# Strassen's scheme for 18 of the 22 k-tiles of each feed-forward down step, in a two-block fp32 transformer kernel on one core

## The chip, the core and the metric

The kernel runs on one core of a Trainium2 chip. The metric is the device time of one execution in microseconds. TensorE (PE) multiplies, VectorE (DVE), ScalarE (ACT) and GpSimd (POOL) do elementwise work, SyncE (SP) issues the DMAs. Each engine works through its own queue in program order, and semaphores tie the queues together.

## The reference

Two blocks of two layers each on 512 tokens of width 1024, all in fp32. What matters here is the last part of each layer:

```python
def conv_ffn(x, w_up, conv_k, conv_b, w_down):           # layers 0 and 1 of the first block
    h = x @ w_up                                         # 1024 -> 2 x 2816
    ...
    h = sum(hp[:, j:j + S] * conv_k[j] for j in range(CONV_W)) + conv_b
    a, b = jnp.split(h, 2, axis=-1)
    return (jax.nn.gelu(a, approximate=False) * b) @ w_down

def swiglu(xn, w_gate, w_up, w_down):                    # layers 0 and 1 of the second block
    return (jax.nn.silu(xn @ w_gate) * (xn @ w_up)) @ w_down
```

In the first block x = layer_norm(ALPHA * x + h) follows, in the second h + swiglu(...). The hidden width 2816 is 22 tiles of 128. The other stages (two mixers, cross attentions, a sparse attention, a convolution module) are not touched.

## The kernel before

**Precision.** Each fp32 operand is split into a high and a low part in the matmul's 32-bit format (`xh`, `xl`; `ah`, `al`; `wh`, `wl`), and each product is three matmuls: high x high, high x low, low x high. ScalarE makes the high part by a copy, VectorE the low part by a subtraction.

**The script.** `Script` writes one list of items; each engine's program goes through the list and does its own part of each item. So the order of the items is the order of every queue. Weights come in units of up to 1024 columns: SyncE loads a unit into one of 3 raw buffers (`weights`, L2391), `split` makes its parts in a ring of NR = 5 slots (L1430 on ScalarE, L1785 on VectorE, recorded at L1438/L1444 and L1792/L1798), and TensorE uses it in `mm` (L1182). `prefetch` (L209) puts the split of unit i + 4 into the list when unit i comes up; ScalarE then waits until unit i - 1 has been used. SyncE issues the load of a later raw unit only when `w_lo` of the present one has been made.

**PSUM.** There are eight banks of 128x512. `take` and `give` hand them out first in, first out; TensorE opens a bank only when its last reader has signalled (`free`).

**The feed-forward step** (`ffn`, L592). Stage numbers si are 2 and 5 in the first block (the conv form, called conv layers below) and 8 and 11 in the second (the gated form, gated layers). An up product `ups(m)` makes hidden tiles m and m + 1 (a pair) from four outputs of 128x512: 4 units of 24 matmuls. Its evacuation in a conv layer is ScalarE's tap (L1592), two taps on VectorE for each output (L2033, L2036), a Gelu, and two products (L2043); then ScalarE makes the hidden tiles' high parts (L1602) and VectorE their low parts (L2048), in `ah` and `al`. In a gated layer ScalarE applies Silu (L1611) and VectorE multiplies (L2056). The order is: six up products; `residual` over hidden tiles 0 to 9; five up products; `residual` over tiles 10 to 21. `residual` (L333) goes through the two halves of the 1024 output columns, four token tiles each, and adds each finished 128x512 sum into `x` (L1995, a first one with ALPHA at L1992). The last half goes token tile by token tile over its last three units, so that layer norms (L1812 to L1821) and transposes (L1196) of the first tiles start early. `by_tiles` (L367) does this for both halves in the cross attention.

## Time and profile before

| | us |
|---|---|
| median of 3 runs | 3467.57 (3466.55 to 3467.74) |
| profiled execution, its own span | 3464.9 |
| TensorE busy | 3404.4 |
| VectorE busy | 1870.3 |
| ScalarE busy | 1401.5 |
| GpSimd busy | 252.1 |
| DMA, mean rate | 91 GB/s |

The busy time of TensorE counts overlapping matmuls once, so its share says whether the queue had work, not how fast that work went. The four feed-forward stages take about 350 us each. Times inside a stretch are from the span's start. PEclk 1.00 is 2.4 GHz.

### The profile page before, as it was taken

How to read it: one execution, taken by the hardware profiler on the slowest of the kernel's cores; microseconds unless marked ns; L12 is line 12 of the kernel's file. 1: busy time of each engine (PE TensorE's matmuls, PEld its weight loads, DVE VectorE, ACT ScalarE, POOL GpSimd, SP SyncE). 2: the span in 40 equal slices, each digit the busy share in tenths (PEclk: the TensorE clock that was granted, in tenths of full speed). 3: DMA queues.
4: the chain of work that ended last, by engine and by line, in shares of the span. 5: the costliest groups of instructions: out<-in, count | busy, mean ns of one | idle time of the engine just before them, and what ended most of it. 6: DMA issues, size and time to landing. Idle time of an engine off the chain costs nothing.

```text
span 3464.9 us, 41693 instructions
## 1 busy us (share of the span) xinstructions
PE 3404.4 (98%) x16871; PEld 2849.4 (82%) x16871; DVE 1870.3 (54%) x3030; ACT 1401.5 (40%) x2489; POOL 252.1 (7%) x319
## 2 busy tenths in 40 slices
PE   9999999999999999999999999999999999999999
PEld 8888888888888888888888777888888887888887
DVE  5644566646565545676455695553333696543332
ACT  4543233424235333334243554544232565543231
POOL 1300210000032002000001020100000000100000
PEclk9999999999999999999999999999999999999999
DMA  4111342322331123423232222412222302313222
GB/s 160 56 55 62 109 158 73 104 97 92 98 105 60 49 86 114 141 68 103 98 98 77 75 71 90 132 57 96 98 97 98 104 28 90 105 55 108 95 96 79
DMA packets 89330, 315.13 MB, mean 91 GB/s; under 512 B 10673, under 2 KB 11441, under 8 KB 88625
## 3 DMA queue, kind: packets, MB, share of 16 engines
q1 hardware_dynamic: 89136, 312.46, 27.4%
q8 instruction: 133, 2.18, 0.3%
q14 instruction: 61, 0.49, 0.0%
HBM read 308.23 MB, written 4.19 MB: 90 GB/s over the span
## 4 chain that ended last, share of the span: by engine, by line
PE 88%; DVE 7%; ACT 2%; POOL 2%; issue 1%; DMA 0%; SPq 0%; DVEq 0%; ACTq 0%; POOLq 0%
PE bk L1182 76%; PE bk L1276 3%; PE bk L1240 2%; PE bk L1250 1%; PE bk L1196 1%; DVE ar L2165 1%; DVE wl L1792 1%; DVE st L2163 1%; PE bk L1367 1%; PE bk L1365 1%; PE bk L1366 1%; POOL x L2354 1%; POOL st L2286 1%; DVE x L1821 0%; DMA wr<-in_wpk 0%
## 5 line engine op out<-in xcount | busy, mean ns | idle before, releaser
L1182 PE MATMUL bk<-xh,wh 128*128 128x512 f32 (+1 forms) x2216 | 837.8, 378 | 5.1 <-DVE xl L1805 5.1
L1182 PE MATMUL bk<-xh,wl 128*128 128x512 f32 (+1 forms) x2216 | 830.3, 375 | 0.0
L1182 PE MATMUL bk<-xl,wh 128*128 128x512 f32 (+1 forms) x2216 | 829.6, 374 | 0.0
L1792 DVE TENSOR_TENSOR wl<-wr,wh 128x1024 fp32r<-128x1024 f32 (+1 forms) x372 | 449.4, 1218 | 660.7 <-ACT wh L1438 659.7
L1438 ACT ACTIVATE wh<-wr 128x1024 fp32r<-128x1024 f32 (+1 forms) x372 | 385.8, 1046 | 706.4 <-PE bk L1182 653.6
L1182 PEld LDWEIGHTS bk<-xh,wh 128*128 128x128 f32 x2216 | 417.5, 188 | 78.6 <-DVE wl L1798 3.8
L1182 PEld LDWEIGHTS bk<-xh,wl 128*128 128x128 f32 x2216 | 417.2, 188 | 75.3
L1182 PEld LDWEIGHTS bk<-xl,wh 128*128 128x128 f32 x2216 | 417.6, 188 | 72.0
L1182 PE MATMUL bk<-wh,ah 128*128 128x512 f32 x1184 | 466.6, 394 | 4.5 <-DVE al L2250 2.9
L1182 PE MATMUL bk<-wh,al 128*128 128x512 f32 x1184 | 461.7, 390 | 0.0
L1182 PE MATMUL bk<-wl,ah 128*128 128x512 f32 x1184 | 461.3, 390 | 0.0
L1798 DVE SCALAR_TENSOR_TENSOR wl<-wr,par,wh 128x512 fp32r<-128x512 f32 (+1 forms) x360 | 249.4, 738 | 308.2 <-ACT wh L1444 306.9
L1444 ACT ACTIVATE wh<-wr,par 128x512 fp32r<-128x512 f32 (+1 forms) x360 | 236.1, 708 | 335.8 <-PE bk L1182 328.8
L1182 PE MATMUL bk<-wh,xh 128*128 128x512 f32 (+1 forms) x768 | 295.6, 385 | 6.3 <-DVE wl L1792 6.3
L1182 PE MATMUL bk<-wh,xl 128*128 128x512 f32 (+1 forms) x768 | 289.4, 377 | 0.0
L1182 PE MATMUL bk<-wl,xh 128*128 128x512 f32 (+1 forms) x768 | 289.2, 377 | 0.0
L1182 PEld LDWEIGHTS bk<-wh,ah 128*128 128x128 f32 x1184 | 222.5, 188 | 51.9 <-issue 3.6
L1182 PEld LDWEIGHTS bk<-wh,al 128*128 128x128 f32 x1184 | 222.4, 188 | 46.5
L1182 PEld LDWEIGHTS bk<-wl,ah 128*128 128x128 f32 x1184 | 222.6, 188 | 45.5 <-issue 0.7
L2286 POOL TENSOR_SCALAR st<-st 128x1 f32<-128x1 f32 (+3 forms) x97 | 48.6, 502 | 2434.6 <-DVE st L1814 988.3
L1276 PE MATMUL bk<-ar 128*128 128x64 f32 (+2 forms) x1168 | 176.1, 286 | 11.9 <-ACT ar L1531 7.6
L1182 PEld LDWEIGHTS bk<-wh,xh 128*128 128x128 f32 x768 | 146.9, 191 | 34.1 <-DVE wl L1792 6.7
(276 smaller groups left out, 4095.5 us busy)
## 6 DMA issues: line engine op xcount, KB each, us to landing
wr<-in_wpk SPq DMA_DIRECT2D x540, 512.0 KB, 3.4
gb<-in_ln_g SPq DMA_DIRECT2D x6, 512.0 KB, 4.5
gb<-in_ln_b SPq DMA_DIRECT2D x6, 512.0 KB, 6.0
ar<-in_xT SPq DMA_DIRECT2D x8, 256.0 KB, 6.5
wr<-in_wpk SPq DMA_DIRECT2D x8, 256.0 KB, 6.0
ar<-in_memT SPq DMA_DIRECT2D x2, 1024.0 KB, 5.0
x<-in_x SPq DMA_DIRECT2D x4, 512.0 KB, 5.3
park<-x SPq DMA_DIRECT2D x4, 512.0 KB, 6.2
```

Of the source, the lines that this page charges most:

```text
L1182: i = pe.e.matmul(dst, lw, rw, start=g not in opened, stop=end)
L1196: i = pe.e.transpose(ps[:, tile(q)], src[:, tile(j + q)], ident)
L1240: ins = pe.e.matmul(ps[:, 0:w], lw, rw, start=q == 0, stop=q == len(pairs) - 1)
L1250: ins = pe.e.transpose(ps[:, tile(q)], src[:, tile(q)], ident)
L1276: ins = pe.e.matmul(ps[:, col:col + A.dv], src[:, tile(q)], val, start=q == 0, stop=k == k1 - 1)
L1365: pe.e.matmul(ps[:, :], dh, oh[:, j:j + 512], start=j == 0, stop=False)
L1366: pe.e.matmul(ps[:, :], dh, ol[:, j:j + 512], start=False, stop=False)
L1438: act.e.activation(m.wh[:, s, 0:nk * cols], m.wr[:, r, 0:nk * cols], ACT.Copy) \
L1444: act.e.activation(m.wh[:, s, a], m.wr[:, r, a], ACT.Copy, scale=m.p(gain[0], gain[1] + kk, 1)) \
L1792: dve.e.tensor_tensor(m.wl[:, s, a], m.wr[:, r, a], m.wh[:, s, a].bitcast(F32), ALU.subtract) \
L1798: i = dve.e.scalar_tensor_tensor(m.wl[:, s, a], m.wr[:, r, a], m.p(gain[0], gain[1] + kk, 1), m.wh[:, s, a].bitcast(F32), ALU.mult, ALU.su ...
L2286: pool.e.tensor_scalar(out, var, scale, eps, ALU.mult, ALU.add).then_inc(*ev.up("pool_ev"))
```

## The change

Hidden tiles 0 to 17 (nine pairs, three phases of three pairs) are multiplied with their weights by seven products in place of eight; a product takes two token tiles, one k-tile combination and 512 columns. Each product has two units: the first with two pairs (12 matmuls), the second with the third pair (6). The order is 1, 2, 5, 6, 3, 7, 4. Four pairs of banks (a to d) hold the sums: products 6 and 7 are added to 1's banks and 3 to 5's, after each state has been read; `sev` adds a state of a bank to one quarter of `x`, or to two (product 7). The combinations of weights (`combo`, T1 to T4) and of the hidden state (`comb`) are made on VectorE. The down weights of the 18 tiles come by `down_load`, 1 MB for a pair, into `wd`, and no longer through the raw ring; the loads of a phase stand in the up product before it, at its last three steps. `hid_hi` and `hid_lo` make the hidden state's parts from a queue `soon`; a pair's seven blocks are 1792 columns. The products' units are put between the units of the next up products: two behind the second, third and fourth unit of a phase's first up product, two behind each unit of its second, and in the third phase three behind some. The last two pairs (tiles 18 to 21) follow in `last_pairs`, both halves, token tile by token tile. The core of the diff:

```diff
+LEFT = {1: 0, 5: 4, 2: 2, 6: 5, 3: 6, 7: 1, 4: 3}
+RIGHT = {1: 0, 5: 1, 2: 2, 6: 1, 3: 3, 7: 0, 4: 2}
+COMBO = {5: "T1", 6: "T2", 7: "T3", 4: "T4"}
+ORDER = (1, 2, 5, 6, 3, 7, 4)
+HOME = {1: "a", 6: "a", 7: "a", 5: "b", 3: "b", 2: "c", 4: "d"}
+PART = {1: ((0, 0),), 5: ((1, 1),), 2: ((0, 0),), 6: ((0, 1),), 3: ((0, 1),), 7: ((1, 1), (1, 0)), 4: ((1, 0),)}
+AFTER = {6: 1, 7: 6, 3: 5}
...
+        units = self.plan or self.units
+        while self.split < min(i + 1 + LOOK, self.rel + NR, len(units)):
+            if units[self.split][0] == "seven":
+                _, F, q, c = units[self.split]
+                for pair in F.chunks[c] if q in COMBO else ():
+                    self.add("combo", F, COMBO[q], pair)
             self.add("split", self.split)
...
+    def seven(self, F):
+        n = len(F.chunks)
+        for q in ORDER:
+            if HOME[q] not in F.home:
+                F.home[HOME[q]] = [self.take(), self.take()]
+            for c in range(n):
+                F.slot[q, c] = self.use(("seven", F, q, c))
+                self.add("smm", F, q, c)
+                self.rel += 1
+                self.prefetch(F.slot[q, c])
+                if c < n - 1:
+                    yield
+            for tt in range(2):
+                self.add("sev", F, q, tt)
+                if q in (2, 3, 7, 4):
+                    self.give(F.home[HOME[q]][tt])
+            yield
...
+        def part(t, u):
+            for G in halves:
+                if u == 0:
+                    G.grp.append(self.take())
+                    if t == 0:
+                        G.unit[0] = self.use((0, 2, G.pieces, None))
+                elif t == 0:
+                    G.unit[1] = self.use((2, 2, G.pieces, None))
+                self.add("mm", G, u, [t], None, t == NT - 1)
+                if t == NT - 1:
+                    self.rel += 1
+                    self.prefetch(G.unit[u])
+        def finish(t):
+            if si == 11:
+                for hf, G in enumerate(halves):
+                    self.add("ev", G, t)
+                    self.give(G.grp[t])
+                    self.add("store", hf, t)
+                return
+            self.add("ev", halves[0], t)
+            self.give(halves[0].grp[t])
+            if t < 2:
+                self.close(si, t)
+            elif t == 2:
+                self.turn_x(si, 0)
+                self.leave(2)
+        for t in range(2):
+            part(t, 0)
+        yield
+        for t in range(2):
+            part(t, 1)
+            finish(t)
+            yield
+        for t in range(2, NT):
+            for u in range(2):
+                part(t, u)
+            finish(t)
+            yield
+        if si != 11:
+            late = [("ln", si, 2), ("turn", si, 2), ("norm", si, 3)] if si in (2, 5) else \
+                [("ln", si, 2), ("norm", si, 3), ("turn", si, 2)]
+            self.rest = [("turn", si, 1)] + late + [("turn", si, 3)]
...
-        for m in range(0, 12, 2):
-            drive((ups(m), 1))
-        drive((self.residual(si, down, [l, 0], 10, "hid", norm=False), 1))
-        for m in range(12, 22, 2):
-            drive((ups(m), 1))
-        drive((self.residual(si, down, [l, 10], 12, "hid", first=False, base=10), 1))
+        def made(pair, seven=None, per=(0, 0, 0, 0), after=0, loads=None):
+            for step, _ in enumerate(ups(2 * pair)):
+                if loads is not None and step in (1, 2, 3):
+                    self.add("down_load", *loads, 3 * loads[0].ph + step - 1, l)
+                if seven is None:
+                    if self.soon:
+                        self.add(*self.soon.pop(0))
+                elif step < 2 and pair % 3 == 0 and self.soon:
+                    self.add(*self.soon.pop(0))
+                for _ in range(per[step] if seven else 0):
+                    next(seven, None)
+            if pair < 9:
+                self.add("comb", si, pair)
+            self.soon += [("hid_hi", si, pair), ("hid_lo", si, pair)]
+        F = [Seven(si, ph, range(3 * ph, 3 * ph + 3)) for ph in range(3)]
+        made(0)
+        made(1, loads=(F[0], None))
+        made(2)
+        for ph in range(3):
+            products = self.seven(F[ph])
+            pair = 3 * ph + 3
+            made(pair, products, (0, 2, 2, 2) if ph < 2 else (0, 3, 3, 2))
+            if ph < 2:
+                made(pair + 1, products, (2, 2, 2, 2))
+                drive((products, 1))
+                made(pair + 2, loads=(F[ph + 1], F[ph]))
+            else:
+                held, self.soon = self.soon, []
+                steps = ups(2 * pair + 2)
+                for step in range(4):
+                    next(steps)
+                    if step < 2:
+                        for _ in range(3):
+                            next(products, None)
+                    if step == 1:
+                        drive((products, 1))
+                        self.soon = held
+                    elif self.soon:
+                        self.add(*self.soon.pop(0))
+                drive((steps, 1))
+                self.soon += [("hid_hi", si, 10), ("hid_lo", si, 10)]
+        while self.soon:
+            self.add(*self.soon.pop(0))
+        drive((self.last_pairs(si, down, l), 1))
...
+    def smm(F, q, c):
+        j = F.slot[q, c]
+        pe.wait_ge(*ev["w_lo", j])
+        for tt in range(2):
+            g = F.home[HOME[q]][tt]
+            ps = bk[sc.bank[g]]
+            if g not in opened:
+                begin(g)
+            if q in AFTER:
+                pe.wait_ge(*ev["sev", F.si, F.ph, AFTER[q], tt])
+            for kk, pair in enumerate(F.chunks[c]):
+                pe.wait_ge(*ev["hid", F.si, pair])
+                a = slice(tt * 128, tt * 128 + 128)
+                hh, hl = (m.hid(side, pair, LEFT[q], 256)[:, a] for side in (m.hh, m.hl))
+                wh, wl = (side[:, j % NR, kk * 512:kk * 512 + 512] for side in (m.wh, m.wl))
+                whole = c == len(F.chunks) - 1 and kk == len(F.chunks[c]) - 1
+                for n, (lw, rw) in enumerate(((hh, wh), (hh, wl), (hl, wh))):
+                    i = pe.e.matmul(ps[:, :], lw, rw, start=g not in opened, stop=whole and n == 2, skip_group_check=True)
+                    opened.add(g)
+            names = [("grp7", F.si, F.ph, q, tt)] if whole else []
+            if tt:
+                names.append(("used", j))
+            if names:
+                i.then_inc(*ev.up("mm", *names))
...
+    def split_seven(j):
+        _, F, q, c = sc.units[j]
+        act.wait_ge(*ev["used", j - NR])
+        for pair in F.chunks[c]:
+            act.wait_ge(*ev[(COMBO[q], F.si, pair) if q in COMBO else ("d_sw", F.si, pair)])
+        n = F.at(c)[1]
+        act.e.activation(m.wh[:, j % NR, 0:n * 512].rearrange("p (k c) -> p k c", k=n), m.right(F, q, c), ACT.Copy) \
+            .then_inc(*ev.up("w_hi", ("w_hi", j, 0)))
+    def hid_hi(si, pair):
+        if pair >= 3:
+            act.wait_ge(*ev["grp7", si, pair // 3 - 1, 4, 1])
+        if pair >= 9:
+            for p in range(2):
+                act.wait_ge(*ev["prod", si, 2 * pair + p])
+            act.e.activation(m.hid(m.hh, pair, 0, 1024), m.z(si, pair), ACT.Copy) \
+                .then_inc(*ev.up("x_hi", ("hid_hi", si, pair)))
...
+    def comb(si, pair):
+        z, zx = heads(m.z(si, pair), 4), heads(m.zx[pair % 2], 3)
+        for p in range(2):
+            dve.wait_ge(*ev["prod", si, 2 * pair + p])
+        if pair >= 2:
+            dve.wait_ge(*ev["hid", si, pair - 2])
+        dve.e.tensor_tensor(zx[:, 0, :], z[:, 1, :], z[:, 3, :], ALU.add).then_inc(*ev.up("dve_ev"))
+        own()
+        dve.e.tensor_tensor(zx[:, 1, :], zx[:, 0, :], z[:, 0, :], ALU.subtract).then_inc(*ev.up("dve_ev"))
+        dve.e.tensor_tensor(z[:, 1, :], z[:, 0, :], z[:, 1, :], ALU.subtract).then_inc(*ev.up("dve_ev"))
+        own()
+        dve.e.tensor_tensor(zx[:, 2, :], z[:, 2, :], zx[:, 1, :], ALU.subtract) \
+            .then_inc(*ev.up("dve_ev", ("comb", si, pair)))
+    def hid_lo(si, pair):
+        dve.wait_ge(*ev["hid_hi", si, pair])
+        i = dve.e.tensor_tensor(m.hid(m.hl, pair, 0, 1024), m.z(si, pair), m.hid(m.hh, pair, 0, 1024).bitcast(F32),
+                                ALU.subtract)
+        if pair >= 9:
+            i.then_inc(*ev.up("x_lo", ("hid", si, pair)))
+            return
+        dve.e.tensor_tensor(m.hid(m.hl, pair, 4, 768), m.zx[pair % 2], m.hid(m.hh, pair, 4, 768).bitcast(F32),
+                            ALU.subtract).then_inc(*ev.up("x_lo", ("hid", si, pair)))
+    def combo(F, name, pair):
+        w = m.wd[:, F.pairs.index(pair)]
+        dst, x, y = {"T1": (1, 1, 0), "T2": (1, 3, 1), "T3": (0, 1, 0), "T4": (2, 2, 1)}[name]
+        if name == "T1":
+            dve.wait_ge(*ev["d_sw", F.si, pair])
+        else:
+            dve.wait_ge(*ev["w_lo", F.slot_of({"T2": 5, "T3": 1, "T4": 2}[name], pair)])
+            dve.wait_ge(*ev["T1" if name == "T2" else "T2", F.si, pair])
+        dve.e.tensor_tensor(w[:, dst, :], w[:, x, :], w[:, y, :], ALU.subtract) \
+            .then_inc(*ev.up("dve_ev", (name, F.si, pair)))
+    def sev(F, q, tt):
+        ps = bk[sc.bank[F.home[HOME[q]][tt]]]
+        dve.wait_ge(*ev["grp7", F.si, F.ph, q, tt])
+        names = [("sev", F.si, F.ph, q, tt)]
+        if q in (2, 3, 7, 4):
+            names.append(("free", F.home[HOME[q]][tt]))
+        for n, (half, hf) in enumerate(PART[q]):
+            t = 2 * half + tt
+            xs = m.x[:, t, hf * 512:hf * 512 + 512]
+            marks = names if n == len(PART[q]) - 1 else []
+            own()
+            if F.si < 6 and F.ph == 0 and (q in (1, 5, 6) or (q, hf) == (7, 0)):
+                i = dve.e.scalar_tensor_tensor(xs, xs, ALPHA, ps[:, :], ALU.mult, ALU.add)
+            else:
+                i = dve.e.tensor_tensor(xs, xs, ps[:, :], ALU.add)
+            i.then_inc(*ev.up("dve_ev", *marks))
...
+    def down_load(F, before, pair, l):
+        n = F.pairs.index(pair)
+        if before is None:
+            sp.wait_ge(*ev["act", F.si, 0])
+        else:
+            sp.wait_ge(*ev["w_lo", before.slot_of(4, before.pairs[n])])
+        sp.e.dma_start(m.wd[:, n].rearrange("p b c -> p (b c)"), ins["wdn"][(F.si // 6 * 2 + l) * 9 + pair, :, :]) \
+            .then_inc(*ev.up(f"d_sw{n}", ("d_sw", F.si, pair), by=16))
```

On SyncE `split` and `weights` skip the units of the products; ScalarE's evacuation of a conv up product waits for the low part two pairs back, as before. `lay_out` packs the down weights of tiles 0 to 17 as pairs.

## Rows read from the trace of the kernel before

**Rows 1.** The page's first part: busy time, share of the span, instructions of each engine.
```profile
span 3464.9 us, 41693 instructions
...
PE 3404.4 (98%) x16871; PEld 2849.4 (82%) x16871; DVE 1870.3 (54%) x3030; ACT 1401.5 (40%) x2489; POOL 252.1 (7%) x319
```

**Rows 2.** The page's chain that ended last, shares of the span by engine.
```profile
PE 88%; DVE 7%; ACT 2%; POOL 2%; issue 1%; DMA 0%; SPq 0%; DVEq 0%; ACTq 0%; POOLq 0%
```

**Rows 3.** Waits of TensorE, whole span: total us, times, longest us.
```profile
PE bk L1196 <- DVE x L1821: 7.7, 8, 1.2
...
PE bk L1182 <- DVE wl L1792: 6.6, 3, 5.7
```

**Rows 4.** Stretches, a conv and a gated feed-forward: length, busy us, clock, DMA share, GB/s.
```profile
591.00:940.00 349.00, 348.96 (x1602) 291.45 (x1600) 188.49 (x226) 125.83 (x155) 3.62 (x4) 1.00 0.31 101
...
2355.00:2690.00 335.00, 335.00 (x1508) 278.79 (x1507) 122.02 (x161) 104.96 (x150) 0.47 (x2) 1.00 0.30 99
```

**Rows 5.** Timeline of TensorE in a down step: start us, us, instruction; 33 matmuls apart.
```profile
2500.06 0.39 PE L1182 MATMUL bk<-wh,al 128*128 128x512 f32 x1
...
2507.54 0.39 PE L1182 MATMUL bk<-wh,al 128*128 128x512 f32 x1
```

**Rows 6.** Timeline of VectorE, evacuation of one conv up product and two splits.
```profile
646.57 0.74 DVE L2033 SCALAR_TENSOR_TENSOR ar<-bk,par,ar 128x511 f32<-128x511 f32 x1
...
652.49 1.29 DVE L2043 TENSOR_TENSOR ar<-ar 128x512 f32<-128x512 f32 x2
...
655.43 2.36 DVE L1792 TENSOR_TENSOR wl<-wr,wh 128x1024 fp32r<-128x1024 f32 x2 [0.26 <-ACT wh L1438]
```

**Rows 7.** Groups of VectorE by form, whole span: count, busy us, mean ns, idle before.
```profile
L1792 DVE TENSOR_TENSOR wl<-wr,wh 128x1024 fp32r<-128x1024 f32 x364 | 444.0, 1229 | 654.2 <-ACT wh L1438 653.2
...
L1995 DVE TENSOR_TENSOR x<-x,bk 128x512 f32<-128x512 f32 x80 | 54.8, 685 | 63.7 <-PE bk L1182 61.2 <-DVE x L1995 0.5
...
L1870 DVE TENSOR_TENSOR al<-bk,ah 128x256 fp32r<-128x256 f32 x16 | 6.8, 425 | 0.5
```

**Rows 8.** ScalarE: two groups by form, whole span, and one row of its timeline.
```profile
L1438 ACT ACTIVATE wh<-wr 128x1024 fp32r<-128x1024 f32 x364 | 380.8, 1055 | 699.2 <-PE bk L1182 653.6 <-DMA wr<-in_wpk 45.5
...
L1602 ACT ACTIVATE ah<-ar 128x512 fp32r<-128x512 f32 x44 | 27.2, 633 | 51.8 <-DVE ar L2043 51.8
...
645.64 0.78 ACT L1592 ACTIVATE ar<-bk,par 128x512 f32<-128x512 f32 x1 [0.24 <-PE bk L1182]
```

**Rows 9.** The page's DMA issues: count, KB each, median us from issue to landing.
```profile
wr<-in_wpk SPq DMA_DIRECT2D x540, 512.0 KB, 3.4
...
ar<-in_memT SPq DMA_DIRECT2D x2, 1024.0 KB, 5.0
```

**Rows 10.** A stretch at the kernel's start, its last column the GB/s.
```profile
8.00:12.00 4.00, 4.00 (x12) 3.15 (x11) 3.11 (x5) 2.42 (x4) 0.00 (x0) 1.00 1.06 412
```

**Rows 11.** Waits of TensorE from 930 to 975, the end of a conv layer.
```profile
PE bk L1196 <- DVE x L1821: 2.2, 2, 1.2
```

**Rows 12.** Stretches in attention; the third number from the right is the granted clock.
```profile
114.40:117.40 3.00, 1.63 (x11) 1.26 (x12) 2.59 (x9) 2.45 (x5) 2.83 (x4) 1.00 0.00 0
117.40:120.80 3.40, 2.70 (x10) 2.01 (x9) 1.74 (x5) 1.74 (x5) 3.22 (x4) 0.50 0.44 124
...
1059.50:1062.90 3.40, 3.40 (x10) 2.63 (x9) 2.18 (x5) 2.11 (x6) 1.25 (x2) 0.50 0.37 145
```

**Rows 13.** Timeline of TensorE at the kernel's start, 12 matmuls between the last two rows.
```profile
5.67 0.79 PE L1182 MATMUL bk<-wh,xh 128*128 128x512 f32 x1 [5.67 <-DVE wl L1792]
6.26 0.63 PE L1182 MATMUL bk<-wl,xh 128*128 128x512 f32 x1
...
11.38 0.50 PE L1182 MATMUL bk<-wl,xh 128*128 128x512 f32 x1
```

More of the change, by code:

```diff
@@ L193, in __init__ @@
         self.last_gate, self.last_branch, self.conv_g = {}, {}, None
+        self.soon = []
         self.build()
+        self.raws = [j for j, d in enumerate(self.units) if d[0] != "seven"]
+        self.raw = {j: r for r, j in enumerate(self.raws)}
     def add(self, *item):
@@ L211, in prefetch @@
             return
-        n = len(self.units) if self.total is None else self.total
-        while self.split < min(i + 1 + LOOK, self.rel + NR, n):
+        units = self.plan or self.units
[4 more added lines that the diff above has]
+                    self.add("combo", F, COMBO[q], pair)
             self.add("split", self.split)
@@ L1455, in rms @@
         else:
-            act.wait_ge(*ev["res", si, 1, t])
+            for hf in range(2):
+                act.wait_ge(*ev["res", si, hf, t])
         if t >= 2 and si > 5:
@@ L2407, in split @@
     def split(j):
-        if j + NRAW < len(sc.units):
+        if j in sc.raw and sc.raw[j] + NRAW < len(sc.raws):
             sp.wait_ge(*ev["w_lo", j])
-            weights(j + NRAW)
+            weights(sc.raw[j] + NRAW)
     def row(name, l, n):
```

116 lines of the change are left out of this document (72 added, 44 removed).

## Prediction

> **What bounds the kernel now.** I read the busy table first: TensorE is busy for 3404.4 of 3464.9 us, VectorE for 1870.3, ScalarE for 1401.5 [rows 1]. The chain that ended last agrees: 88% of it is TensorE [rows 2]. The list of who waited for whom shows how little TensorE waits for others: the two largest causes are 7.7 and 6.6 us [rows 3]. So removed matmuls pay, but only as far as the other queues keep pace, and the next view is the table of the feed-forward stretches. In the first block's ones (conv, si 2 and 5) VectorE works 188.5 of 349 us and ScalarE 125.8; in the second block's (gated, si 8 and 11) 122.0 and 105.0 of 335 [rows 4]. TensorE has no gap in either. A 512-column matmul there follows the one before it after (2507.54 - 2500.06) / 33 = 0.2267 us [rows 5]; its listed 0.39 us is latency, not price. A unit of 24 matmuls thus lasts 5.44 us, and an up product (4 units) 21.8 us.
>
> **What is removed.** Before, 9 pairs of k-tiles in the down step cost 9 x 2 x 8 x 3 = 432 matmuls in each of 4 layers; seven products on two token tiles cost 9 x 7 x 2 x 3 = 378. So 54 x 0.2267 = 12.24 us a layer, **49.0 us in all**. The last 4 of 22 k-tiles keep their count.
>
> **What is added, by price.** Matmul forms are the same. On VectorE, per layer: 36 differences of weights (T1 to T4) of 128x512, which follow each other after 0.60 us (two end within 1.29 [rows 6]); 36 differences of the hidden state at 256 columns, 0.42 us each by the nearest form, 9 x 1.6 = 14 us [rows 7]; low halves for 1792 instead of 1024 columns a pair, 9 x 0.85 = 8 us; 46 weight splits (25 full at 1.13 us in a row, 21 half at 0.60 [rows 6]) instead of 22, +16 us; 48 + 8 readings of sums into x instead of 16, each 0.69 [rows 7] plus the wait on its own queue, 0.72, +29 us. With 22 us for the weights this is about +89 us a layer: 188 to 277 of some 340 us in the conv layers, 122 to 211 in the gated ones. On average there is room. The order decides, so I walked one phase (3 pairs) through the in-order queues.
>
> VectorE's lead is the ring of 5 split weights: unit i+4 is split while TensorE works on unit i. A product has only two units, of 12 and 6 matmuls (2.72 and 1.36 us), so four units of lead shrink from 21.8 us to 13.6 to 16.3. For products 4 to 7 the split is serial: differences (1.2 us), ScalarE's copy 1.06 (half: 0.63 [rows 8]), VectorE's subtraction 1.15.
>
> **Conv layers, first phase.** Time 0 is the start of the first woven up product. The first woven up lasts with its 3 products to 34.0, the second with 4 products to 72.1, the free third to 93.8. VectorE is idle last near 24, then it works to the end of the second: 7.2 us for each up product's taps and products (646.57 to 653.8 [rows 6]), 11 splits, 14 sum readings of 0.72, 9 differences, 1.6 us of hidden differences. It frees the first bank that the second woven up reuses at about 31.9, where TensorE asks at 34.0; it splits the unit asked for at 43.5 by 40.7. These margins of 2 to 3 us hold, so **no stall** inside (estimate; 0 to 3 us a phase is the bound). But it lags: it splits the second unit of the next phase's first up at 82.3, where an unburdened queue would at 79.9.
>
> **Change of phase.** SyncE's in-order queue passes that split, then issues one weight transfer and at once all three 1 MB transfers of the next phase's weights: the units between are products, for which it doesn't wait. One 512 KB transfer lands after 3.4 us, a 1 MB one after 5.0 [rows 9], and at 412 GB/s [rows 10] a further 1 MB takes 2.6, by the difference in rows 9 3.2. The second lands at 82.3 + 3.4 + 2 x (2.6 to 3.2) = 91 to 92, the third at 93.5 to 95.3. ScalarE meets the splits of these weights at 83 and stands; behind them in its queue is the evacuation of the third up, whose first bank is complete at 89.8. That starts 4 to 6 us late. From the third landing: copy 0.6, tap 0.8, VectorE's 7.2, low half of the pair before 2.0, hidden differences 1.6, high half 1.85, a weight copy 1.0 and its split 1.15, low half 2.0: 18.2 us, so 111.7 to 113.5. TensorE asks for this pair in the first product's second unit, at 107.4. **Stall 4.3 to 6.1, taken 5.3**, twice a layer; without the transfers it would be about 0.1. In the gated layers the same walk has 79.8 for SyncE, no taps, and ends at 105.1, before 107.4: no stall.
>
> **Third phase.** Its weave puts the second product's last unit right ahead of product 5, which takes the banks that product 2 gives back. VectorE reads them only behind two differences and a split. TensorE asks 1.36 us after the unit's start; the readings end 2.3 us too late in conv layers (1.5 to 3), 1.8 in gated ones (1.2 to 2.4).
>
> **Ahead of the last two pairs.** The low half of pair 9 stands in VectorE's queue behind pair 10's evacuation, and the first matmul after that up asks for it. In the trace the first output's tap begins at 645.64, a quarter into the last unit [rows 8], so the up ends near 649.6, the products end at 653.8, and the low half needs another 1.15: **5.4 us** (5.0 to 6.0). Gated: one multiply 0.7, low half 1.15, signals: 2.1 (1.8 to 2.6). Pair 10 itself is ready at +6.5, behind 5.44 us of matmuls that start at +5.4: hidden.
>
> **The tail by token tile.** From the first tile's end to its transposes there are 36 matmuls, as before. VectorE has one reading and its statistics more for each tile; the present order waits 2.2 us in that place [rows 11]. I take +1 in the two conv layers (0 to 2) and nothing in the gated ones, the last store included.
>
> **TensorE's clock.** The table of stretches shows a granted clock of 1.00 (2.4 GHz) from 114.4 to 117.4, while TensorE was busy 1.63 of 3 us, and 0.50 (1.2 GHz) over the next 3.4; another fall lasts 3.4 us in all [rows 12]. At the kernel's start the matmuls behind a pause of 5.67 us follow each other after (11.38 - 6.26) / 12 = 0.427 us [rows 13], and only from 11.4 on at the full pace. So a fall of 3.4 us costs 3.4 x (1 - 0.2267 / 0.427) = 1.6 us. The six pauses of over 5 us (three in each conv layer) can each be followed by one: 0 to 9.6 us, taken at 6.4 (four of six). The Trainium skill, page "TensorE: Matmul & The Clock Gate", section "HAM oscillation — how this bites in real kernels", says that long idle gaps between groups of matmuls put the array back to its low clock. By that rule all six would be paid, and the sum would be 3 us higher.
>
> A second rule speaks against the change: the skill's page "VectorE: DVE Perf Modes", section "The TRN2 errata — SBUF-src ops pay a fixed extra latency per instruction", has small operands pay the same fixed part as large ones. The trace has it: 0.42 us for 256 columns and 0.69 for 512 [rows 7]. With the page's formula, (N + 151) / 0.96 ns, an estimate for the four hidden differences of a pair is 1.7 us instead of 1.6, which changes nothing.
>
> **The sum.** Conv layer: 2 x 5.3 + 2.3 + 5.4 + 1 = 19.3, two layers 38.6. Gated: 1.8 + 2.1 = 3.9, two 7.8. Clock 6.4. Together 52.8 lost against 49.0 removed: +3.8 us. The profiled execution spans 3464.9 us, the median of the three runs shown is 3467.6, 2.7 us longer, and I keep that distance: **3471 us**. With all lower ends (8.6 a phase pair, 1.5, 5.0, 0; gated 3.0; no clock) the loss is 36.2 us and the time 3455, with all upper ones (12.2, 3, 6, 2; gated 5.0; 9.6) it is 66 and 3485.
>
> **Rivals.** *The gain is kept.* If ScalarE meets the new weights already landed, the phase stall falls to 0.1 (minus 20.8 us), and with it most of the clock term (minus 5) and the tail (minus 2): 3443 us. For it: my walk gives VectorE's lag to within a microsecond or so, and the three transfers would only need to be issued 5 us earlier. Against it: SyncE's place behind that split is in the code. Chance 0.33 for this and what lies between (3438 to 3462).
> *VectorE becomes the bound.* In the second woven up of every conv phase the margin is 2.1 us at the first reused bank. A phase adds 44 instructions in VectorE's queue up to 72 (12 differences, 14 product splits, 14 readings, 4 of the hidden state). If each costs 0.12 us more than here, for a handshake with ScalarE or a wait on its own queue, that is 5.3 us a phase, of which the margin takes 2.1: 3.2 x 6 phases = 19, so 3490 us, slower. It decides from 2.1 / 44 = 0.05 us an instruction. For it: every price here was seen on a VectorE about half busy. Against: back to back instructions in rows 6 run closer than their listed time. Chance 0.25 (3479 to 3500).
> The forecast, 3462 to 3479, has 0.38; 0.04 lies outside. That the change doesn't do what it says I leave out: the matmul count is fixed by the code.
>
> What a measurement of this kernel can tell from no change is about 0.2%, 7 us. Faster by more (under 3460.6): the first rival, almost whole, and an edge of the forecast, 0.35. Slower by more (over 3474.5): the second and a part of the forecast, 0.32. Between: 0.33. The range that leaves out 2 in 10 runs from 3441 to 3489; the likeliest case's own from 3462 to 3479.
>
> **What would show it.** 216 fewer matmuls. Waits of TensorE on the low halves (the hidden state's, in the second unit of a phase's first product): 4 of about 5 us; one of 5.4 in each conv layer ahead of the last pairs, 2.1 in each gated one; one of about 2 us in each layer on the sum readings. ScalarE idle 5 to 8 us behind a transfer at each change of phase. Stretches at clock 0.50 behind the 5 us pauses. VectorE about 277 us busy in a conv layer. The prediction is wrong if TensorE waits on split weights inside a phase (then the second rival), or if ScalarE doesn't stand at the changes of phase (then the first).

## The result, and the profile after

| | us |
|---|---|
| before, median of the runs beside it | 3467.06 |
| after, median of 4 runs | 3493.49 (3492.06 to 3494.12) |
| ratio, 95% interval | 1.0076 [1.0062, 1.0091] |
| profiled execution after, its own span | 3490.3 |

The kernel became slower by 26 us. That is 22.5 us above the forecast of 3471, 4.5 us above the upper end of the wide range (3489), and well beyond the 7 us that the prediction took as the least change that can be told from none.

The first lines of the page of the kernel after, and the shares of its chain; they answer to [rows 1] and [rows 2]:

```profile
span 3490.3 us, 42076 instructions
...
PE 3372.2 (97%) x16655; PEld 2815.0 (81%) x16655; DVE 2205.2 (63%) x3566; ACT 1475.6 (42%) x2577; POOL 252.3 (7%) x319
...
PE 41%; DVE 5%; ACT 1%; issue 1%; POOL 0%; ACTq 0%; DVEq 0%; POOLq 0%
```

The 216 matmuls are gone (16871 to 16655), and VectorE has 335 us more work. The shares of the chain in this view add up to only 48% of the span, so TensorE's 41% can't be held against the 88% of before, and nothing is sized by it. The waits of TensorE over the whole span do have sizes (total us, times, longest us), to be held against [rows 3]:

```profile
PE bk L1369 <- DVE al L2017: 27.4, 8, 5.4
PE bk L1344 <- DVE al L2012: 14.8, 4, 5.4
PE bk L1344 <- DVE xl L2070: 9.3, 9, 1.6
PE bk L1344 <- DVE wl L2057: 8.8, 4, 6.2
PE bk L1383 <- DVE x L2086: 7.9, 8, 1.3
...
PE bk L1369 <- DVE x L2045: 7.0, 4, 1.7
```

L1369 is the matmul of a product, L1344 that of nearly everything else. Three causes are new: the low halves behind the hidden differences (L2017), which are the changes of phase; the low half of pair 9 (L2012); and the readings of sums into `x` (L2045), which are the third phase's reused bank. Together 49.2 us, already as much as the 49.0 that the removed matmuls save.

The clock of TensorE comes on top. Stretches of the kernel after, around the first change of phase (length, busy us with counts for TensorE, its loads, VectorE, ScalarE, GpSimd, granted clock, DMA share, GB/s):

```profile
752.60:758.60 6.00, 4.82 (x21) 3.67 (x20) 5.90 (x10) 0.42 (x2) 0.00 (x0) 1.00 0.00 1
758.60:760.60 2.00, 0.39 (x2) 0.00 (x0) 0.72 (x1) 2.00 (x3) 0.00 (x0) 1.00 0.15 16
760.60:764.30 3.70, 0.00 (x0) 0.00 (x0) 3.32 (x4) 1.82 (x3) 0.00 (x0) 0.54 0.36 133
764.30:771.30 7.00, 6.94 (x24) 5.68 (x25) 5.13 (x7) 1.06 (x1) 0.00 (x0) 0.75 0.25 75
2709.90:2713.30 3.40, 3.40 (x9) 2.70 (x9) 1.05 (x2) 0.00 (x0) 0.00 (x0) 0.51 0.32 105
```

TensorE starts nothing between 758.6 and 764.3, the granted clock falls to its lower level (1.2 GHz) inside that pause, and work resumes while it is still low. Summed over the whole span the clock was low for 61.4 us, against 23.9 before.

TensorE's timeline behind the pause, the same kernel (start us, us, instruction, idle before and its releaser):

```profile
764.36 0.77 PE L1369 MATMUL bk<-wh,ah 128*128 128x512 f32 x1 [5.37 <-DVE al L2017]
764.92 0.63 PE L1369 MATMUL bk<-wl,ah 128*128 128x512 f32 x1
765.35 0.63 PE L1369 MATMUL bk<-wh,al 128*128 128x512 f32 x1
765.78 0.63 PE L1369 MATMUL bk<-wh,ah 128*128 128x512 f32 x1
```

They follow each other after 0.43 us, as in [rows 13], not after 0.2267 [rows 5]. All six pauses of over 5 us, and one of 2.0 in a gated layer (the last stretch above, clock 0.51), were followed by such work, 26.7 us of it, which costs 26.7 x (1 - 0.2267 / 0.427) = 12.5 us.

So the span: 49.2 + 12.5 - 49.0 = +12.7 from what is named. The small waits grew by another 8.3 (on the low halves of `x`, L2070, 9.3 us against 6.4; on weight splits 8.8 against 6.6 [rows 3]; the rest in attention and the transposes). The row of before for the low halves of `x`:

```profile
PE bk L1182 <- DVE xl L1805: 6.4, 7, 1.1
```

A wait costs a little more than its row says. The row counts from the end of the matmul before, 0.39 us after its start, while the next one would have started 0.2267 us after it: 0.16 us more for each wait. The kernel after has 86 waits in this view, the one before 65, which makes an estimated 3.4 us. The whole is 3490.3 - 3464.9 = +25.4, so about 1 us is left without a name. By stage: the conv feed-forwards, from first to last matmul, went from 383.7 to 400.9 and from 383.1 to 402.5, the gated ones from 365.2 to 358.8 and from 363.3 to 355.3, and all else by +3.0. The change pays in the gated layers and loses in the conv layers. The stages that it doesn't touch are a part of the 3.0: ahead of the first feed-forward alone (0 to 578) the waits on weight splits are 8.3 us against 6.6.

### The profile page after: what moved, and what is told of

Its sections match the earlier page's. It is cut to its first block and busy times, and to the rows that moved or that the text cites. A ratio compares the mean times of both kernels' runs of the same rounds, so it can differ in the third digit from the quotient of the medians.

```text
span 3490.3 us, 42076 instructions
## 1 busy us (share of the span) xinstructions
PE 3372.2 (97%) x16655; PEld 2815.0 (81%) x16655; DVE 2205.2 (63%) x3566; ACT 1475.6 (42%) x2577; POOL 252.3 (7%) x319
## 5 line engine op out<-in xcount | busy, mean ns | idle before, releaser
L1344 PE MATMUL bk<-xh,wh 128*128 128x512 f32 (+1 forms) x2216 | 838.3, 378 | 5.7 <-DVE xl L2070 5.6
L1344 PE MATMUL bk<-xh,wl 128*128 128x512 f32 (+1 forms) x2216 | 830.3, 375 | 0.0
L1344 PE MATMUL bk<-xl,wh 128*128 128x512 f32 (+1 forms) x2216 | 830.0, 375 | 0.0
L2057 DVE TENSOR_TENSOR wl<-wr,wh 128x1024 fp32r<-128x1024 f32 (+1 forms) x300 | 361.9, 1215 | 302.4 <-ACT wh L1650 301.1
L1344 PEld LDWEIGHTS bk<-xh,wh 128*128 128x128 f32 x2216 | 418.0, 189 | 79.8 <-issue 4.1
L1344 PEld LDWEIGHTS bk<-xh,wl 128*128 128x128 f32 x2216 | 417.6, 188 | 75.6
L1344 PEld LDWEIGHTS bk<-xl,wh 128*128 128x128 f32 x2216 | 418.0, 189 | 72.1
L1650 ACT ACTIVATE wh<-wr 128x1024 fp32r<-128x1024 f32 (+1 forms) x300 | 310.2, 1043 | 313.8 <-PE bk L1344 218.7
L1623 ACT ACTIVATE wh<-ar 128x1024 fp32r<-128x1024 f32 (+1 forms) x168 | 141.1, 843 | 487.0 <-DVE ar L2028 271.0
L1993 DVE TENSOR_TENSOR wl<-ar,wh 128x1024 fp32r<-128x1024 f32 (+1 forms) x168 | 160.6, 958 | 231.3 <-ACT wh L1623 231.1
L1344 PE MATMUL bk<-wh,xh 128*128 128x512 f32 (+1 forms) x768 | 294.8, 384 | 11.7 <-DVE wl L2057 8.6
L1344 PE MATMUL bk<-wl,xh 128*128 128x512 f32 (+1 forms) x768 | 288.1, 375 | 0.0
L1344 PE MATMUL bk<-wh,xl 128*128 128x512 f32 (+1 forms) x768 | 288.0, 375 | 0.0
L1344 PE MATMUL bk<-wh,ah 128*128 128x512 f32 x608 | 244.9, 403 | 19.2 <-DVE al L2012 14.8
L1344 PE MATMUL bk<-wh,al 128*128 128x512 f32 x608 | 239.2, 393 | 0.0
L1344 PE MATMUL bk<-wl,ah 128*128 128x512 f32 x608 | 239.1, 393 | 0.0
L1369 PE MATMUL bk<-wh,ah 128*128 128x512 f32 x504 | 199.9, 397 | 34.3 <-DVE al L2017 27.4
L1369 PE MATMUL bk<-wl,ah 128*128 128x512 f32 x504 | 198.5, 394 | 0.0
L1369 PE MATMUL bk<-wh,al 128*128 128x512 f32 x504 | 198.4, 394 | 0.0
```

The lines of the kernel that those rows point to most:

```text
L1344: i = pe.e.matmul(dst, lw, rw, start=g not in opened, stop=end)
L1369: i = pe.e.matmul(ps[:, :], lw, rw, start=g not in opened, stop=whole and n == 2, skip_group_check=True)
L1623: act.e.activation(m.wh[:, j % NR, 0:n * 512].rearrange("p (k c) -> p k c", k=n), m.right(F, q, c), ACT.Copy) \
L1650: act.e.activation(m.wh[:, s, 0:nk * cols], m.wr[:, r, 0:nk * cols], ACT.Copy) \
L1993: dve.e.tensor_tensor(part(m.wl), m.right(F, q, c), part(m.wh).bitcast(F32), ALU.subtract) \
L2057: dve.e.tensor_tensor(m.wl[:, s, a], m.wr[:, r, a], m.wh[:, s, a].bitcast(F32), ALU.subtract) \
```

## The experiments

My theory after the traces: VectorE has room enough; the loss is three places where the order of a queue makes TensorE wait, and the clock's falls behind these pauses. The rival: VectorE, with 89 us more a layer, is the bound, and a wait that is cured comes back elsewhere. Below, each place is undone alone first, then all three, then the two halves of the theory (clock, VectorE's room) are tried by themselves. Differences in microseconds are between medians, and "after" is the changed kernel; the kernel before, run beside each, stayed at 3467.0 to 3467.3.

### The next phase's loads earlier

```diff
-                if loads is not None and step in (1, 2, 3):
+                if seven is None and loads is not None and step in (1, 2, 3):
                     self.add("down_load", *loads, 3 * loads[0].ph + step - 1, l)
+                if seven is not None and loads is not None and step == 3:
+                    for n in range(3):
+                        self.add("down_load", *loads, 3 * loads[0].ph + n, l)
...
-                made(pair + 1, products, (2, 2, 2, 2))
+                made(pair + 1, products, (2, 2, 2, 2), loads=(F[ph + 1], F[ph]))
                 drive((products, 1))
-                made(pair + 2, loads=(F[ph + 1], F[ph]))
+                made(pair + 2)
```

> The three 1 MB loads of the next phase stand one up product earlier, behind the last unit of the phase's second up product; nothing else changes. Handover theory: ScalarE no longer stands behind a transfer, so TensorE's waits on the hidden state at the changes of phase, 27.4 us in the changed kernel (27.4 in 8 waits), fall to under 4 us, and the low-clock stretches behind them in the conv layers (four of 6.8, 3.4, 6.8 and 6.8 us) go: about -24 and -10 us, so 3457 to 3465 us. Rival, VectorE is the bound of the conv layers: the queue is late anyway, the waits move to split weights or to the low halves of the hidden state and the time stays above 3480 us.

Measured: 3460.04 us, ratio to the kernel before 0.9981 [0.9971, 0.9990], 33 us less than after, as the handover theory expected. The waits of TensorE in this kernel (L2015 is pair 9's low half, L2048 the readings):

```profile
PE bk L1347 <- DVE al L2015: 14.8, 4, 5.4
...
PE bk L1372 <- DVE x L2048: 8.2, 4, 2.5
```

The 27.4 us on the low halves at the changes of phase are down to 0.7, and the clock was low for 44.4 us instead of 61.4. SyncE issued the three loads at 718.24; in the kernel after it did at 733.22. So the place of these loads in SyncE's queue alone carries 33 us, more than the 26 by which the change is slower.

### The low half of pair 9 ahead of the next evacuation

```diff
-                    elif self.soon:
+                    while step == 2 and self.soon:
                         self.add(*self.soon.pop(0))
```

> Only the low half of pair 9 moves ahead of pair 10's evacuation in VectorE's queue. Handover theory: the wait ahead of the last two pairs (5.4, 5.4, 2.0, 2.0 us) goes; instead pair 10's low half is late by about 1 us in the conv layers. With the low-clock stretches behind the pauses (6.8, 6.8 and 3.4 us) that is -13 and -8 us: 3470 to 3476 us. Rival, VectorE is the bound: what is moved forward delays the evacuation by as much, and the time falls by under 4 us.

Measured: 3473.05 us, 1.0018 [1.0009, 1.0028], 20.4 less than after. The waits on pair 9's low half are gone; what is left on L2012 is pair 10's, 1.2 us in each conv layer, as expected. The list keeps the other two causes:

```profile
PE bk L1369 <- DVE al L2017: 26.8, 8, 5.4
...
PE bk L1369 <- DVE x L2045: 7.0, 4, 1.7
...
PE bk L1344 <- DVE al L2012: 2.4, 2, 1.2
```

12.4 us of waiting were cured for 20.4 us of time. The falls of the clock behind these pauses are gone as well (low for 44.4 us); in the kernel after they held 11.3 us of work, which by the same sum is 5.3 us. Some 3 us are left open.

### The third phase's weave

```diff
-            made(pair, products, (0, 2, 2, 2) if ph < 2 else (0, 3, 3, 2))
+            made(pair, products, (0, 2, 2, 2) if ph < 2 else (0, 2, 2, 4))
```

> The changed kernel with the third phase's first weave as 0, 2, 2, 4 in place of 0, 3, 3, 2. Handover theory: TensorE's four waits of 1.7 us on the readings into x go and nothing else: 3486 to 3488 us. Rival, VectorE is the bound: the readings come no earlier and the time stays above 3491 us.

Measured: 3482.91 us, 1.0048 [1.0033, 1.0063], 10.6 less, where I had some 7, so 3 us beyond the expected range. The 7.0 us on the readings are gone; the low halves stand at 25.5, 1.9 less, and all waits together fell by 11.5 (113.2 to 101.7), the remaining 2.6 in small ones. The clock gave nothing back: it was low for longer here (68.3 us). Since the five runs lie between 3480.2 and 3487.7, the 3.6 us beyond 7 are not more than their spread.

### All three

> Both edits, and in the third phase the weave 0, 2, 2, 4 in place of 0, 3, 3, 2, so that an up unit stands between product 2's reading and product 5. Handover theory: of the 49 us removed about 8 are lost to small waits and tails; 3424 to 3436 us, no low-clock stretch inside a feed-forward. Rival, VectorE is the bound: at least 18 us stay in the conv layers, 3445 us or more.

Measured: 3431.28 us, **0.9896 [0.9881, 0.9911]**. The three alone gave 33.4, 20.4 and 10.6, in sum 64.4; together they give 62.2, so hardly any cured wait came back elsewhere. The clock was low for 17.1 us, never inside a feed-forward. The whole span's waits and one conv and one gated stretch, to hold against [rows 4]:

```profile
PE bk L1347 <- DVE xl L2073: 9.2, 9, 1.6
PE bk L1466 <- ACT ar L1747: 8.2, 15, 0.9
PE bk L1386 <- DVE x L2089: 8.2, 8, 1.4
PE bk L1347 <- DVE wl L2060: 8.0, 4, 6.2
```

```profile
575.00:945.00 370.00, 364.62 (x1709) 303.81 (x1708) 295.23 (x388) 154.07 (x190) 7.32 (x8) 1.00 0.31 103
2375.00:2720.00 345.00, 343.35 (x1622) 288.63 (x1622) 217.32 (x316) 139.39 (x205) 2.96 (x8) 1.00 0.28 92
```

The list is again that of the kernel before: layer norms, transposes, one weight. The gated layers shrink by 12.25 us each, the full price of the removed matmuls; the conv layers by 6.9, with VectorE busy for 295 of 370 us. What they lack is in many waits of 1 to 2 us (first tile's low halves, one weight, and 1.4 and 1.2 on L2015, the low half ahead of the last pairs), not in one.

### The pauses filled with matmuls

```diff
+    def fill(j, g):
+        ps = begin(g)
+        pe.wait_ge(*ev["w_lo", j])
+        for n in range(22):
+            i = pe.e.matmul(ps[:, :], m.xh[:, n % 8, 0:128], m.wh[:, j % NR, 0:512], start=True, stop=True)
+        i.then_inc(*ev.up("pe_at", ("free", g)))
...
+                if F.si < 6 and F.ph and (q, c) == (1, 1):
+                    self.fill(F.slot[q, c])
...
+                        if si < 6 and G is halves[0]:
+                            self.fill(G.unit[0])
```

> The changed kernel with 22 matmuls of 128 columns stationary and 512 moving put into each of the six pauses of 5.4 us in the conv layers (5.0 us of work into a spare bank whose result nobody reads). Nothing that anyone waits for comes earlier. Clock theory: the granted clock stays at 1.00 behind these pauses and the time falls by what the low clock costs, 15 to 18 us: 3475 to 3479 us. Rival, the pauses alone make the loss and the low clock lies beside other waits: the same 3490 to 3496 us.

The 22 matmuls go into a bank that nobody reads. Measured: 3481.03 us, 1.0039 [1.0025, 1.0053]: 12.5 us less than after, although 132 matmuls were added and no cause of a wait was removed. That refutes the rival of no change; the expected 15 to 18 us were too many. The stretch at the first change of phase of this kernel, where after had 0.54 and 0.75:

```profile
758.00:776.00 18.00, 17.73 (x79) 14.36 (x78) 12.39 (x15) 5.38 (x7) 0.00 (x0) 1.00 0.22 61
```

So the low clock costs time of its own. How much is less sharp than the medians suggest. The execution that was profiled is the slowest of the five (3478.6 to 3485.3), and in it four falls of 3.4 us stay inside the feed-forwards, behind pauses of 2.0 to 2.6 us that weren't filled. They hold 13.4 us of work, 6.3 us by the same sum, so 12.5 - 6.3 = 6.2 us of the clock's price should be gone; its span is 6.8 us shorter than that of after. Execution against execution the count holds; that the medians also differ by 12.5 is chance.

### Where the landing's time comes from

```diff
-        sp.e.dma_start(m.wd[:, n].rearrange("p b c -> p (b c)"), ins["wdn"][(F.si // 6 * 2 + l) * 9 + pair, :, :]) \
+        sp.e.dma_start(m.wd[:, n].rearrange("p b c -> p (b c)")[:, 0:512], ins["wdn"][(F.si // 6 * 2 + l) * 9 + pair, :, 0:512]) \
```

> The changed kernel, but each of the 1024 KB loads of the down weights brings only its first 512 columns (256 KB), at the same place in SyncE's order; what is left of the tile is stale, so part of the down product's weights is not the model's. If the hand-over waits (27.4 us on the low half behind the difference taps, 8 of them) come from the time that the bytes take to land, ScalarE's stand of 12.5 us before wh<-ar shrinks to under 8, these waits shrink to 1 to 2 us each, most falls of the clock behind them go, and the time is 3456 to 3470 us, near that of e1_early_loads (3460). The rival is that the place of the loads in SyncE's order, or VectorE's own backlog at the change of phase, sets them: then the waits keep 5 us each and the time stays at 3485 us or more.

This kernel leaves out three quarters of these weights. Measured: 3475.77 us, 1.0024 [1.0014, 1.0034]. Neither expectation held; the time is 6 us above the first's range and 9 below the second's. TensorE's waits of this kernel, then ScalarE at the first change of phase of the kernel after, then of this one:

```profile
PE bk L1369 <- DVE al L2017: 12.5, 4, 3.5
```

```profile
743.42 1.06 ACT L1623 ACTIVATE wh<-ar 128x1024 fp32r<-128x1024 f32 x1 [12.48 <-DMA ar<-in_wdn]
```

```profile
738.27 1.06 ACT L1623 ACTIVATE wh<-ar 128x1024 fp32r<-128x1024 f32 x1 [8.94 <-DMA ar<-in_wdn]
```

With a quarter of the bytes ScalarE stands 3.5 us less, and the low halves cost TensorE 12.5 us over the four changes instead of 27.4, 3.1 each instead of 6.9: the one was handed on to the other whole. The rest stays, since even the small transfers are issued late and land after 6.0 us, behind two 512 KB ones. So it is both: the place in the queue decides that ScalarE stands, the bytes decide for how long. Only the earlier issue removes all of it.

### Is VectorE the bound?

The first kernel is the changed one with each difference of weights made for one column only; the other 511 are left out:

```diff
-        dve.e.tensor_tensor(w[:, dst, :], w[:, x, :], w[:, y, :], ALU.subtract) \
+        dve.e.tensor_tensor(w[:, dst, 0:1], w[:, x, 0:1], w[:, y, 0:1], ALU.subtract) \
```

> The changed kernel in which each difference of weights (T1 to T4) is computed for one column in place of 512, with all its signals and places in the queues: the rest of the weight combinations is left as loaded, so the result is not the reference's. It takes about 36 x 0.55 = 20 us of VectorE's work out of each layer. VectorE-bound rival: the conv layers get faster by most of it, 40 us in all, under 3460 us. Handover theory: only VectorE's lag at the change of phase shrinks, by at most 2.4 us at each of four changes, and a little at the waits on the readings: 3480 to 3490 us.

Measured: 3490.22 us, 1.0066 [1.0048, 1.0084], 3.3 less than after. The group of the differences in this kernel and, below, in the kernel after (count, busy us, mean ns, idle before):

```profile
L2028 DVE TENSOR_TENSOR ar<-ar 128x1 f32<-128x1 f32 x144 | 18.0, 153 | 0.0
```

```profile
L2028 DVE TENSOR_TENSOR ar<-ar 128x512 f32<-128x512 f32 x144 | 94.6, 685 | 0.0
```

77 us of VectorE's work were taken away and 3.3 came back, at the upper edge of what the handover theory expected. The 3.3 hide two opposite parts: TensorE's waits fell by 7.3 us (113.2 to 105.9, 4.5 of it at the changes of phase), while in the profiled execution more work fell on the low clock, 55.7 us against 45.3 over the whole span, which costs 4.9 more. Even 7.3 of 77 is little: in the kernel after, VectorE is no bound. How much room it has once the waits are gone is shown by the opposite, on the kernel with all three edits: each difference issued twice (where it is made in place, the second one makes the values wrong; the work is what counts here).

```diff
+        dve.e.tensor_tensor(w[:, dst, :], w[:, x, :], w[:, y, :], ALU.subtract).then_inc(*ev.up("dve_ev"))
+        own()
         dve.e.tensor_tensor(w[:, dst, :], w[:, x, :], w[:, y, :], ALU.subtract) \
```

> On the kernel with all three edits (3431.3 us): each difference of weights is computed twice in a row, the second behind a wait on the first (the in-place ones come out wrong): 36 x 0.72 = 26 us more on VectorE in each layer, 8.6 us a phase. By the margin worked out ahead of the change (2.1 us at the first reused bank of a phase) the conv layers lose 6 x 6 = 36 us or more: 3460 us and above. If VectorE's queue had more room than that, under 3440 us. Gated layers: nothing.

Measured: 3469.75 us, 1.0008 [0.9998, 1.0017], 38.5 more than with all three. The expectation had 12 more instructions a conv phase, 0.69 us each, 8.2 us, less the 2.1 us of margin that I had walked: 6.1, in six phases 37. The waits of this kernel:

```profile
PE bk L1347 <- DVE wl L2062: 13.7, 5, 6.0
...
PE bk L1347 <- DVE al L2015: 7.3, 2, 3.7
PE bk L1372 <- DVE al L2020: 6.6, 4, 3.2
PE bk L1347 <- DVE ar L2306: 5.3, 6, 0.9
```

The time agrees with the 37, but the parts don't. In the two conv layers TensorE's waits sum to 37.0 us, with all three edits alone to 13.3: 24 us more, 4 a phase and not 6.1. Another 12 us are the clock: 25.5 us of work in the feed-forwards at the low pace, where the kernel with all three edits has none. (The profiled execution, 3474.49 us, is the slowest of the ten.) So the margin was about 4 us a phase (8.2 - 4), not 2.1, and the 38.5 met the 37 by luck. The first reused bank of a phase (L2306 reads it) does wait, at 684.43 where the second woven up starts, but only in the first phase of each conv layer and for 0.8 us; the other four of the six stand in the free third ups. The largest waits are in the third phase, 3.4 on a split weight and 3.7 on a low half. Each gated layer got one new wait on the readings, 1.0 and 1.3 us, where I had expected none.

Last, the same differences by GpSimd, again on the kernel with all three edits (`combo` moved whole from VectorE's program into GpSimd's):

```diff
-        dve.e.tensor_tensor(w[:, dst, :], w[:, x, :], w[:, y, :], ALU.subtract) \
-            .then_inc(*ev.up("dve_ev", (name, F.si, pair)))
+        pool.e.tensor_tensor(w[:, dst, :], w[:, x, :], w[:, y, :], ALU.subtract) \
+            .then_inc(*ev.up("pool_ev", (name, F.si, pair)))
```

> On the kernel with all three edits: the differences of weights on GpSimd in place of VectorE, 22 us a layer off VectorE, 36 x about 1.26 = 45 us on GpSimd. Handover theory: VectorE isn't the bound there, so -4 to +1 us, 3427 to 3432 us. If VectorE still sets the conv layers, -8 us or more. If the two engines disturb each other at the memory, VectorE's own instructions get longer and the time rises by 3 us or more.

Measured: 3429.30 us, **0.9891 [0.9876, 0.9907]**, 2.0 less than with all three; the intervals overlap, the runs' ranges (3429.04 to 3429.54 and 3430.31 to 3431.54) don't. GpSimd's group, and two of VectorE's, of this kernel; then the same two with all three edits alone:

```profile
L2547 POOL TENSOR_TENSOR ar<-ar 128x512 f32<-128x512 f32 x144 | 210.5, 1487 | 917.3 <-DMA ar<-in_wdn 515.8 <-DVE wl L1996 401.5
L1996 DVE TENSOR_TENSOR wl<-ar,wh 128x1024 fp32r<-128x1024 f32 x84 | 110.3, 1314 | 48.2 <-ACT wh L1626 48.2
L1996 DVE TENSOR_TENSOR wl<-ar,wh 128x512 fp32r<-128x512 f32 x84 | 61.8, 736 | 125.7 <-ACT wh L1626 125.7
```

```profile
L1996 DVE TENSOR_TENSOR wl<-ar,wh 128x1024 fp32r<-128x1024 f32 x84 | 102.8, 1224 | 86.7 <-ACT wh L1626 86.5
L1996 DVE TENSOR_TENSOR wl<-ar,wh 128x512 fp32r<-128x512 f32 x84 | 58.1, 692 | 86.6 <-ACT wh L1626 86.6
```

Both means mix two cases. Two instructions of this kernel that meet, GpSimd's and VectorE's (start us, us):

```profile
676.91 2.28 POOL L2547 TENSOR_TENSOR ar<-ar 128x512 f32<-128x512 f32 x1
675.86 2.18 DVE L1996 TENSOR_TENSOR wl<-ar,wh 128x1024 fp32r<-128x1024 f32 x1
```

96 of the 144 subtractions on GpSimd take 1.3 us, the others up to 2.3. Of VectorE's 84 splits of 1024 columns the 12 that overlap one take 1868 ns in the mean, the other 72 take 1221 as without it. So nothing gets evenly slower: a few instructions get longer by up to 1 us where the two engines meet, and that stays hidden. Taking the differences off VectorE shortened each conv layer by only some 0.4 us, so with all three edits VectorE's load isn't what holds it either. This is the fastest version, 38 us under the kernel before.

## Why the prediction was wrong, point by point

**What bounds, and what is removed: right.** TensorE alone, 216 matmuls at 12.24 us a layer. With the waits gone the gated layers give back 12.25.

**Change of phase: mechanism right, size short.** Every link of the walk is there, and each of the early ones comes later than predicted. Phase time 0, the start of the first woven up, is 649.9 in this trace: the first product's matmul starts at 660.79, two units of 5.44 us behind it. SyncE's issue: predicted 82.3, measured 733.22, or 83.3. ScalarE released by the second load: predicted 91 to 92, measured 743.42, or 93.5; it had stood for 12.5 us, where I had 5 to 8. The copy behind the third load: predicted 93.5 to 95.3, measured 746.07, or 96.2. From there the chain takes 18.1 us, predicted 18.2, and the low half is ready at 764.2, or 114.3, instead of 111.7 to 113.5. ScalarE's copy, then VectorE in the kernel after, in that stretch:

```profile
746.07 0.61 ACT L1623 ACTIVATE wh<-ar 128x512 fp32r<-128x512 f32 x1
...
753.30 1.29 DVE L2308 TENSOR_TENSOR ar<-ar 128x512 f32<-128x512 f32 x2
754.51 1.22 DVE L2012 TENSOR_TENSOR al<-ar,ah 128x1024 fp32r<-128x1024 f32 x1
755.64 0.95 DVE L2017 TENSOR_TENSOR al<-ar,ah 128x768 fp32r<-128x768 f32 x1
756.51 0.42 DVE L2002 TENSOR_TENSOR ar<-ar 128x256 f32<-128x256 f32 x1
...
763.26 0.95 DVE L2017 TENSOR_TENSOR al<-ar,ah 128x768 fp32r<-128x768 f32 x1
```

The step that failed is the arrival of the third load: SyncE's issue came 1.0 us later than the walk had it, and from issue to copy it took 12.9 us, near the top of the 11.2 to 13.0 that the walk had for the third transfer. TensorE's question was placed right: with no wait it would have asked for this low half at 757.35 (754.63 and 12 matmuls), or 107.4. It started at 764.36, 7.0 us later, where I took 5.3 and had 6.1 as the upper end. In the rows this stands as two waits, 1.2 on the low half of pair 4, which the product's first unit needs, and 5.4 on that of pair 5. I had not asked for pair 4 at all, but that isn't what it cost: pair 5's low half comes at 764.2 whatever TensorE did before, so without the first wait the second would have been as much longer. Four changes cost 27.4 in the rows instead of 21.2: **+6.2 us** mis-sized. The kernel with a quarter of the bytes bears this out: its issue is at 83.3 too, ScalarE goes on at 89.9, and TensorE starts 3.4 us late in one single wait.

**Bank of the third phase: right**, a little large in the conv layers (1.7 in each of four layers, 7.0 in all, against 2.3 and 1.8, 8.2 in all). **Pair 9: right**, 5.4 and 2.0 (14.8 in all, 15.0 predicted).

**Clock: the term mis-sized most by ratio.** I took four falls of 1.6 us, 6.4. It was seven, at the pauses named above, and TensorE worked at the low pace for 26.7 us: 12.5, **+6 us**. What failed first is the number: six long pauses and not four (+3.2), and a fall behind a pause of 2.0 us, which I hadn't counted at all (+1.6). The price of one was short as well (+1.3 over six): I took each fall to hold 3.4 us of work, and the six held 3.1 to 5.0. Five of the six lasted 6.8 us, part of it still inside the pause. The kernel before had shown falls longer than 3.4: the one of [rows 12] went on,

```profile
120.80:124.20 3.40, 3.40 (x10) 2.63 (x9) 3.32 (x7) 0.80 (x2) 0.26 (x1) 0.50 0.08 30
```

and another lasted 10.2 us from 2080.1. Even all six at 1.6, my upper bound of 9.6, was short. The Trainium skill's rule that I had weighed (page "TensorE: Matmul & The Clock Gate", section "HAM oscillation — how this bites in real kernels", long idle gaps put the array back to its low clock) is borne out: in or behind all six long pauses the clock fell. I had not followed it in full.

**What I left out.** The tail was given +1 a conv layer. The waits of small size grew by 8.3 us in the whole kernel, among them those on the low halves of `x`, also in stages that the change doesn't touch; each of 21 more waits costs 0.16 us beyond its row, 3.4; and about 1 us has no name. Beyond the tail's 2 the prediction had nothing for this, it was put at zero without a reason: **some +11 us**, the largest single part of the miss. Which queue makes each small wait I haven't followed. Together 6.2 + 6 + 11, less the 1.2 by which the bank's term was too large, are 22: that is the distance from 3471 to 3493.

**VectorE's load: right.** Predicted +89 us a layer; the whole kernel has 335 more, 84 a layer. The stretches of the kernel after from first to last matmul, which are longer than those that the predicted 277 and 211 us were added up for, show:

```profile
578.00:965.00 387.00, 364.19 (x1686) 302.95 (x1684) 289.33 (x380) 151.00 (x187) 7.32 (x8) 0.98 0.28 95
2375.00:2733.00 358.00, 353.19 (x1652) 296.06 (x1652) 215.51 (x311) 140.92 (x197) 2.96 (x8) 1.00 0.29 96
```

**The rivals.** *VectorE becomes the bound* gave 3490, the nearest figure, for a cause that the runs refute: 77 us less of its work bring 3.3 us. That its number was near is luck. Its margin was about twice the 2.1 us that it named, as the doubled differences show. *The gain is kept* named the right cure: loads issued 5 us earlier. Its 3443 took 28 us off the forecast; measured from after, the earlier loads took off 33. **The range** was too narrow at its upper end: each bound was taken from the seen falls and waits, there was none for what the walk didn't name, and the prediction's own bound of 0 to 3 us a phase inside the conv layers was left out of the sum of the upper ends.

## What to carry to other kernels

When matmuls are removed, walk the in-order queues at every hand-over between phases and ask for each operand of each unit when it is made, not for the last one only; a load that SyncE issues behind someone else's split made ScalarE stand for 12 us here, and moving it was worth 33 us. Take the delay of a phase from its last operand, not from the sum of the separate questions. Here a TensorE pause of 5 us cost its length plus about 2 us for the clock, and the small waits together grew by 8.3 us, more than the smallest of the three named causes (7.0). When a number agrees, as the 37 us of the doubled differences did, split it before you believe it. A load on VectorE that looks heavy (295 of 370 us) may cost little where the order is right, so before moving work to another engine take it away once and look at the time.

## What the runs showed of the hardware that I had not expected

- The clock's falls behind pauses of 5.4 us lasted mostly 6.8 us (five of six); and one pause of 2.0 us (matmul starts 2.4 apart, at 2706.1) was followed by one of 3.4, while another of the same length at 3462.2 was not.
- Three 1024 KB loads issued behind two of 512 KB landed in a median of 9.6 us, and 7.8 over the whole kernel, against 5.0 for one alone [rows 9]:

```profile
ar<-in_wdn SPq DMA_DIRECT2D x3, 1024.0 KB, 9.6
wr<-in_wpk SPq DMA_DIRECT2D x2, 512.0 KB, 4.6
```

- GpSimd's subtraction of 128x512 in fp32 takes 1.3 us alone and up to 2.3 when it meets a split of VectorE's, and such a split takes up to 2.2 us instead of 1.2; the means in the rows above (1487 ns, 6 to 7% longer) hide this.
